# GLA heads: the sixth piece of the attention projection is cut into eight k steps and issued between the tiles' products

## The reference, cut to what matters

```
q_d = q * exp(b);  k_d = k * exp(-b)          # b: running sum of the log decay in a chunk of 64
attn = where(causal, q_d @ k_d.T, 0);  o_intra = attn @ v
u = (k * exp(b_last - b)).T @ v               # what a chunk adds to the state
s = d * s + u                                 # the state, chunk after chunk
o = o_intra + q_d @ s_prev
merged = gates[:, :, 0] * (att @ w_proj_attn) + gates[:, :, 1] * (gla @ w_proj_gla)
```

## Time and profile before

| | us |
|---|---|
| time, median of 3 runs | 3081.75 |
| time, lowest and highest | 3071.12, 3092.43 |
| the profiled execution's own time | 3073.72 |
| its span | 3071.8 |
| PE busy in the span | 2759.7 |
| DVE busy | 1317.1 |
| mean granted clock of the profiled execution | 0.933 |

### The profile page before, as it was taken

How to read it: one execution, slowest core, us unless ns; L and a number is a source line. 1 busy time by engine, 2 the same in 40 slices (tenths; PEclk the granted TensorE clock), 3 DMA queues, 4 the chain that set the end, 5 groups by cost and what they waited for, 6 DMA issues and landing times.

```text
span 3071.8 us, 42478 instructions
## 1 busy us (share of the span) xinstructions
PE 2759.7 (90%) x15803; PEld 2394.0 (78%) x15803; DVE 1317.1 (43%) x2797; ACT 690.4 (22%) x1188; POOL 676.0 (22%) x515
## 2 busy tenths in 40 slices
PE   3969999978999999968889999596989999999996
PEld 3968889978888889845556655396988989889894
DVE  5047999972455544213333333622333122222316
ACT  2033211112233443212122322311031101111111
POOL 5212122221100000110000000021343444343333
PEclk9979999989999999978888888698989999999999
DMA  4142322223211111145443332433111111111101
GB/s 186 58 105 54 107 80 88 87 71 90 82 50 58 31 45 42 50 123 157 143 119 112 115 117 99 146 117 130 42 42 42 41 41 53 43 41 41 41 27 58
DMA packets 173659, 244.03 MB, mean 79 GB/s; under 512 B 49890, under 2 KB 147331, under 8 KB 164147
## 3 DMA queue, kind: packets, MB, share of 16 engines
q1 hardware_dynamic: 139890, 204.03, 20.7%
q10 hardware_dynamic: 33600, 37.80, 3.6%
HBM read 180.00 MB, written 59.08 MB: 78 GB/s over the span
## 4 chain that ended last, share of the span: by engine, by line
PE 66%; DVE 18%; issue 6%; DMA 3%; SPq 2%; ACT 2%; POOL 2%; DVEq 2%; POOLq 0%; ACTq 0%; PEldq 0%
PE ps L974 6%; DVE masks L1715 6%; PE ps L1237 4%; PE ps L1238 4%; PE ps L1239 4%; PE ps L1259 4%; PE ps L1258 4%; PE ps L1257 4%; PE ps L854 3%; DVE maskS L1715 3%; PE ps L855 2%; PE ps L856 2%; PE ps L1078 2%; PE ps L962 2%; PE ps L776 2%
## 5 line engine op out<-in xcount | busy, mean ns | idle before, releaser
L411 POOL TENSOR_TENSOR pool_go<-pool_go 128x1 f32<-128x1 f32 x73 | 15.6, 213 | 2156.1 <-PE ps L856 768.9
L2093 DVE TENSOR_TENSOR res<-res,ps 128x512 f32<-128x512 f32 (+1 forms) x270 | 184.6, 686 | 516.7 <-PE ps L1259 516.7
L416 POOL TENSOR_TENSOR w_lo<-raw,w_hi 128x512 fp32r<-128x512 f32 x292 | 376.4, 1322 | 10.5
L854 PE MATMUL ps<-xt_hi,w_hi 128*128 128x368 f32 x768 | 261.5, 341 | 0.6
L855 PE MATMUL ps<-xt_lo,w_hi 128*128 128x368 f32 x768 | 258.1, 336 | 0.0
L1237 PE MATMUL ps<-xt_hi,w_hi 128*128 128x368 f32 x768 | 254.2, 331 | 4.0 <-SPq L368 4.0
L856 PE MATMUL ps<-xt_hi,w_lo 128*128 128x368 f32 x768 | 257.1, 335 | 0.0
L1238 PE MATMUL ps<-xt_lo,w_hi 128*128 128x368 f32 x768 | 254.5, 331 | 0.0
L1239 PE MATMUL ps<-xt_hi,w_lo 128*128 128x368 f32 x768 | 253.9, 331 | 0.0
L1257 PE MATMUL ps<-w_hi,a_hi 128*128 128x512 f32 (+1 forms) x576 | 227.0, 394 | 8.5 <-DVE res L2093 8.5
L1259 PE MATMUL ps<-w_lo,a_hi 128*128 128x512 f32 (+1 forms) x576 | 227.0, 394 | 0.0
(11 more groups left out here) (286 smaller groups left out, 6164.0 us busy)
## 6 DMA issues: line engine op xcount, KB each, us to landing
raw<-w_stream SPq DMA_DIRECT2D x73, 1024.0 KB, 4.9
kpg<-cache_k SPq DMA_DIRECT2D x128, 128.0 KB, 2.2
qT_d<-kT ACTq DMA_DIRECT2D x48, 184.0 KB, 1.9
gate_d<-kT ACTq DMA_DIRECT2D x48, 184.0 KB, 1.9
gst<-gate_d SPq DMA_DIRECT2D x16, 552.0 KB, 5.7
gvog_d<-kT ACTq DMA_DIRECT2D x64, 128.0 KB, 1.9
qraw<-qT_d SPq DMA_DIRECT2D x64, 128.0 KB, 3.1
vpg<-cache_v ACTq DMA_DIRECT2D x64, 128.0 KB, 2.6
```

Of the source, the lines that this page charges most:

```text
L416: last = pool.tensor_tensor(w_lo[:, s, part], raw[:, s, part], w_hi[:, s, part].bitcast(F32), ALU.subtract)
L854: pe.matmul(out, hi, xt_hi[:, k, cols], start=k == 0, stop=False)
```

## The change

The sixth piece (q = 5) is no longer issued in one go ahead of the tiles. `project` gets bounds for k, and the piece's k step n - 1 (three matmuls) is issued in tile n, for n = 1 to 8, right behind `intra(n + 1)`. Because `intra` writes bank 3 in those tiles, the sixth piece moves to bank 7, and waits for the fifth. DVE evacuates it after the tile loop, ahead of the samples' part. SP stores the parts and loads the weight unit after tile 9's output store in place of tile 0's, and loads the next head's gates after that, in place of after tile 3's.

```diff
-                    if n == 0:
+                    if n == 9:
                         sp.wait_ge(pa_ev, 6 * (h + 1))
                         for c in range(2):
                             at0 = P * (2 * h + c)
                             sp.dma_start(part_d[at0:at0 + P, :], gst[:, c, :]).then_inc(pa_out, 16)
                         load_unit(U_PG + h, (U_PG + h) % 2, U_PG + h - 1)
-                    if n == 3 and h + 1 < GH:
-                        sp.wait_ge(pa_out, 32 * (h + 1))
-                        load_head_gates(h + 1)
+                if h + 1 < GH:
+                    sp.wait_ge(pa_out, 32 * (h + 1))
+                    load_head_gates(h + 1)
...
-            def project(h, q):
+            def project(h, q, k0=0, k1=KC):
...
+                if k0 == 0:
+                    if q == 0:
+                        pe.wait_ge(w_split, U_PA + h + 1)
+                    if q == 5:
+                        pe.wait_ge(pa_ev, 6 * h + 5)
+                    elif 6 * h + q >= 2:
+                        pe.wait_ge(pa_ev, 6 * h + q - 1)
+                out, cols = ps[:, 3 if q in (1, 3) else 7, 0:N3], slice(N3 * (q % 3), N3 * (q % 3) + N3)
+                for k in range(k0, k1):
...
-                last.then_inc(unit_done if q == 5 else pa_mm, 1)
+                if k1 == KC:
+                    last.then_inc(unit_done if q == 5 else pa_mm, 1)
...
-                for q in range(2, 6):
+                for q in range(2, 5):
                     project(h, q)
                 pe.wait_ge(ga_ready, h + 1)
...
                     if n == 0:
-                        pe.wait_ge(pa_ev, 6 * (h + 1))
+                        pe.wait_ge(pa_ev, 6 * h + 5)
                     if n < 9:
                         intra(n + 1)
+                    if 1 <= n < 9:
+                        project(h, 5, n - 1, n)
...
                 dve.drain().then_inc(ga_ready, 1)
-                pa_gated(h, 5)
                 order = [OT[8]] + OT[:8] + [OT[9]]
...
                                                      ps[:, 4 + c, 0:DV], ALU.mult, ALU.add).then_inc(ga_s, 1)
+                pa_gated(h, 5)
                 i, at0, r = order[9]
```

More of the change, by code:

```diff
@@ L1932, in pa_gated @@
                 part = gst[:, q // 3, N3 * (q % 3):N3 * (q % 3) + N3]
-                dve.tensor_tensor(part, ps[:, 3 if q % 2 else 7, 0:N3], part, ALU.mult).then_inc(pa_ev, 1)
+                dve.tensor_tensor(part, ps[:, 3 if q in (1, 3) else 7, 0:N3], part, ALU.mult).then_inc(pa_ev, 1)
             dve.memset(reset[:, :], 1.0)
```

## The result

The changed kernel took 3130.07 us (median of four executions, 3112.55 to 3136.87) beside 3077.87 (3071.12 to 3092.43): ratio 1.0154, 95% interval 1.0097 to 1.0212. It is slower, since the whole interval lies above 1. The forecast was 3107 us in a range of 3063 to 3140, also slower; the direction and the range held, the size by the medians came out half as large again (52.2 us for 33.3).

The account below looks back on a forecast made before the run. It took the tile loops to be bound by PE, its granted clock the large term. From 3073.72 us: loops -0.3, start -2.6, handovers +6.0, end +2.5, low heads +27.7, giving 3107 us, range 3063 to 3140.

Parts of the forecast that it names:

- a loop held at 1.00: Tile loop at full clock throughout, with the inserted matmuls: 38.1 + 4.0 = 42.1 us.
- A loop that came back: Tile loop starting at half clock and back at full after two tiles: 48.2 us, expected in two heads of three.
- one that stayed low: Tile loop at half clock not back before tile 9: 69.0 us, 20.8 more, expected in one head of three.
- The end: End of the stage: state stores land behind parts and weight unit, 0 to 4.4 us later, 2.5 taken.
- the count of low loops: Over the four heads' tile loops: one head in three stays low, 4/3 x 20.8 = +27.7 us.
- The gap: PE idle ahead of each tile loop, from the fifth piece's end to the chain's end: 3.3 us.
- start: Ahead of the tiles: without the sixth piece, tiles start 0.65 us earlier a head, -2.6 in four.
- handovers: Between heads: moved stores and loads make gates or inputs late, 2.0 us each, +6.0 in three.
- the move that does nothing: Rival: the sixth piece's move has no effect, as PE's order is not the diff's; 3074 to 3082 us, chance 0.02.
- The held clock: Rival: inserted matmuls bring the clock back at once, every tile loop takes 42.1 us; 3055 us, chance 0.12.
- No return: Rival: the steps never bring the clock back, every tile loop takes 69.0 us; 3162 us, chance 0.10.
- The handover as a mechanism of the time: Rival: serial DMAs at each loop's end set the next head's start; 3116 us, 3130 with two heads low, chance 0.16.

Follow-up runs that it names:

- The second profiled execution: The changed kernel, unaltered, timed again beside the kernel before: median 3140.94 us, ratio 1.0192; its profiled execution took 3126.81 us.
- the kernel with two steps in tile 0: Changed kernel with six of the sixth piece's k steps ahead of the tiles, two in tile 0, stores and loads in earlier tiles: 3057.66 us, ratio 0.9904.
- the gap is filled: Changed kernel plus useless dense matmuls (20 in head 0, 34 in the others) where PE stood idle ahead of the tiles: 3061.22 us, ratio 0.994.
- the stores-only kernel: Kernel before with only SP's part of the change, its stores and loads moved: 3119.1 us; with 13 useless matmuls in heads 1 to 3: 3071.62 us.
- the gap alone: Kernel before, same work and DMAs, fifth piece in bank 6 and sixth in bank 7, so PE's idle time collects ahead of the loops: 3136.17 us, ratio 1.0183.
- one step of eight: Changed kernel with only the last of the sixth piece's eight k steps, in tile 8, the other seven left out: 3147.71 us, ratio 1.0225.
- three steps in tile 0: Changed kernel with five of the sixth piece's k steps ahead of the tiles, three in tile 0, stores and loads in earlier tiles: 3039.16 us, ratio 0.9863.

## Why the prediction was right, and where it was short

**Right in mechanism, point by point.** The sixth piece left its place without making the loop start earlier by more than 0.7 us: head 0 starts 19.61 behind the log decay for 20.30. PE stood idle ahead of every loop, with `ga_ready` its releaser. Every loop of the profiled execution was at half clock within its first microsecond, which is shown to follow from the gap by the two kernels that fill it and that open it alone. The steps cost 0.51 us a tile at full clock (3.82 for 3.31, forecast 0.50), and a loop held at 1.00 took 41.7 us (forecast 42.1). A loop that came back took 47.2 to 47.5 (48.2), and it did so in the second full tile, as forecast; one that stayed low took 70.3 (69.0). The ACT waits for `o_d` in tiles 3 and 4 are gone. The end cost 2.9 (2.5).

**The term that was too small is the count of low loops.** I put one head in three. The profiled execution has one in full and half of a second, and its loops cost 31.0 us in place of 27.4; it is the shortest of its four, and the median is 17.5 us longer, about 0.8 of a low loop. The second profiled execution has two. So about half of the loops stay low rather than a third: 2 x 20.8 in place of 4/3 x 20.8 gives 3107 + 13.9 = 3121 us. The rest up to the two medians, 3130 and 3141, is in executions that were not profiled. Their mean granted clock is lower, 0.916 to 0.919 in the other three of the result for 0.926 in the profiled one, which fits; that it is low loops again is argued from this and from the 23 us steps of the kernel with two steps in tile 0, not shown. My ground for "two in three come back", that the changed tile lies between two rows, was weak: it says that some come back, not how many. That the guess came out near enough for the time to lie in the range is in part luck.

**The gap was 4.8 to 6.0 us, not 3.3.** Two parts. In heads 1 to 3 the handover's delay adds to the gap, since late inputs delay the chain but not the pieces: 3.3 with 2.8, 2.2 and 2.6 us of delay makes 6.1, 5.5 and 5.9, and 6.04, 5.61 and 5.86 were measured. The forecast priced the delay and did not carry it into the gap. In head 0 the fifth piece ended sooner, as it ran at full clock there, where it had run partly at half before.

**The handover was sized nearly right.** Forecast start -2.6 and handovers +6.0, together +3.4; measured +4.8, with the inputs 2.8, 2.2 and 2.6 us late (2.0 forecast) and the gates not late at all. The slack of 1.8 us was the right row to read. As a price by itself it is small beside a low loop; its larger effect is that it widens the gap.

**Of the rivals,** the move that does nothing is out, since the trace has the steps where the diff puts them. The held clock is out: none of the eight loops in the two profiled executions held 1.00. It becomes true in three loops of four once the gap is filled. No return is out as a whole, and true of head 0 in both and of head 2 in the second. The handover as a mechanism of the time is out; as a cause of the gap it is part of the answer, which the stores-only kernel shows (3119 us with the gap, 3072 without). The rule that a busy PE has the full clock (the Trainium skill, TensorE: Matmul & The Clock Gate, "What's actually happening") does not agree with this trace: PE was busy without a break for 11.8 us at 0.50.

## What to carry to other kernels

When a piece of dense work is taken out from ahead of a light stretch, ask first what the engine does in its place: if the next step waits for another engine, nothing is gained but idle time, and here 4.8 us of idle PE ahead of light matmuls halved the clock for the whole stretch behind it. Price a stretch at both granted clocks and look at what stands at its entrance; a few dense matmuls in the lightest spot there (here 1.5 us a head) can be worth far more than they cost. Do not spread them through a stretch that holds its clock by itself, since there each is paid in full (0.51 us a tile).

## What the runs showed of the hardware that was not expected

- The granted clock has a memory through the work itself. The same tiles ran at 1.00 for a whole loop (38.6 us, head 1 of the kernel before) and at 0.50 up to tile 9 (62.0 to 63.6 us, the gap alone), with PE busy for 95% and 98% of the time. The profiled executions of three kernels (the gap alone, one step of eight, SP's part alone) have twelve loops without the steps; all twelve were low, and none came back before tile 9.
- A long gap ahead of a loop made the fall certain here, a short one or none did not exclude it. In the profiled executions of all the kernels, all 17 loops behind 3.4 us or more of idle PE were at 0.50 within their first microsecond. Of the 26 behind 1.5 us or less, 10 fell as well, nine of them 2 to 4 us behind a start at 1.00. What decides among these was not found; with three steps in tile 0 none of the three stayed low.
- The cost can come in steps: the executions of the kernel with two steps in tile 0 differ by 23 us and not by a spread, 3034.71 and 3035.41 beside 3057.03 to 3058.92.
- Whether the steps in the tiles bring the clock back is near the edge here, and yet mostly the same by head: in the second full tile in heads 1 and 3, never in head 0, in both profiled executions alike, while head 2 came back late in one and not in the other. Two executions are few for this, and why head 0 differs was not tried.
